# Three attentions of a decoder trunk's token mixer run as one sequence of 96 steps

## The reference, cut to what matters

```python
y_a = dsa_attention(...)              # keys chosen per query by an indexer's top-k (128 of 512)
y_b = rglru_branch(...)
y_c = mla_attention(...)              # causal, 96-wide heads
y_d = sliding_window_attention(...)   # window 128, a sink per head
ys = jnp.stack([y_a, y_b, y_c, y_d], axis=2)
proj = jnp.einsum('bsnw,nwd->bsnd', ys, w_branch)
g = jax.nn.sigmoid(gates.reshape(B, S, N_BRANCH, D_MODEL))
return jnp.sum(g * proj, axis=2) @ w_out
```

## Time and profile before

| what | value |
|---|---|
| median of 3 runs | 2865.91 us (2855.36 to 2866.02) |
| the profiled execution's own time | 2861.46 us |
| its span, first to last instruction | 2859.7 us |
| mean granted clock of TensorE, as a share of full speed | 0.995 |
| PE busy | 2749.6 us, 96% of the span |
| DVE busy | 1564.8 us, 55% |
| ACT busy | 1107.7 us, 39% |
| POOL busy | 272.9 us, 10% |

### The profile page before, as it was taken

The page is one execution under the profiler, slowest core; times in us unless marked ns, Lnnn a source line. Parts: engine busy times, 40 slices in busy tenths (PEclk is TensorE's granted clock), DMA queues, the critical chain, the costliest instruction groups (busy, mean ns, idle before and its releaser), DMA issues.

```text
span 2859.7 us, 37617 instructions
## 1 busy us (share of the span) xinstructions
PE 2749.6 (96%) x13312; PEld 2214.5 (77%) x13312; DVE 1564.8 (55%) x2636; ACT 1107.7 (39%) x2024; POOL 272.9 (10%) x360
## 2 busy tenths in 40 slices
PE   4999999998999999999999999999999999999999
PEld 4888888676767788888888888877666778888887
DVE  6655446767455647633266653567665466553323
ACT  2322234565454443222242222346555453432222
POOL 0111000112110001110011110001111000011100
PEclk9999999999999999999999999999999999999999
DMA  5655422111212224533335544221112223153332
GB/s 232 231 180 192 143 97 78 54 50 60 67 60 96 89 82 177 197 99 101 96 118 204 192 154 147 98 67 53 59 60 67 74 74 104 52 191 99 93 99 69
DMA packets 86252, 318.54 MB, mean 111 GB/s; under 512 B 9697, under 2 KB 10081, under 8 KB 84706
## 3 DMA queue, kind: packets, MB, share of 16 engines
q1 hardware_dynamic: 86114, 316.76, 32.5%
HBM read 314.62 MB, written 2.10 MB: 111 GB/s over the span
## 4 chain that ended last, share of the span: by engine, by line
PE 83%; DVE 7%; ACT 2%; issue 2%; DVEq 2%; DMA 2%; SPq 0%; POOL 0%; ACTq 0%; POOLq 0%
PE bank L453 19%; PE bank L454 19%; PE bank L455 19%; PE bank L462 6%; PE bank L460 6%; PE bank L461 6%; PE bank L1677 2%; PE bank L1661 1%; DVE w_low L437 1%; PE bank L1650 1%; DMA ada_raw<-ada 1%; PE bank L1642 1%; DVE scores_sb L1152 1%; DVEq L967 1%; ACT w_high L431 1%
## 5 line engine op out<-in xcount | busy, mean ns | idle before, releaser
L453 PE MATMUL bank<-h_high,w_high 128*128 128x512 f32 (+1 forms) x2528 | 976.8, 386 | 21.9 <-DVE h_low L1270 12.2
L455 PE MATMUL bank<-h_high,w_low 128*128 128x512 f32 (+1 forms) x2528 | 958.5, 379 | 0.0
L454 PE MATMUL bank<-h_low,w_high 128*128 128x512 f32 (+1 forms) x2528 | 958.4, 379 | 0.0
L437 DVE TENSOR_TENSOR w_low<-w_raw,w_high 128x1024 fp32r<-128x1024 f32 x437 | 565.8, 1296 | 654.2 <-ACT w_high L431 652.4
L431 ACT ACTIVATE w_high<-w_raw 128x1024 fp32r<-128x1024 f32 x437 | 458.6, 1051 | 356.1 <-PE bank L462 331.6
L453 PEld LDWEIGHTS bank<-h_high,w_high 128*128 128x128 f32 x2528 | 479.2, 190 | 126.2 <-issue 40.7
L455 PEld LDWEIGHTS bank<-h_high,w_low 128*128 128x128 f32 x2528 | 478.5, 189 | 89.6
L454 PEld LDWEIGHTS bank<-h_low,w_high 128*128 128x128 f32 x2528 | 478.6, 189 | 86.4 <-issue 2.4
L460 PE MATMUL bank<-w_high,ffn_high 128*128 128x512 f32 x704 | 275.6, 391 | 0.0
L462 PE MATMUL bank<-w_low,ffn_high 128*128 128x512 f32 x704 | 273.9, 389 | 0.0
L461 PE MATMUL bank<-w_high,ffn_low 128*128 128x512 f32 x704 | 273.9, 389 | 0.0
(11 more groups left out here) (194 smaller groups left out, 2716.7 us busy)
## 6 DMA issues: line engine op xcount, KB each, us to landing
w_raw<-stream SPq DMA_DIRECT2D x440, 512.0 KB, 3.6
ada_raw<-ada SPq DMA_DIRECT2D x128, 512.0 KB, 3.6
ada_start<-ada SPq DMA_DIRECT2D x8, 1024.0 KB, 17.2
mixer_consts<-mixc SPq DMA_DIRECT2D x2, 1152.0 KB, 5.1
x<-x_in SPq DMA_DIRECT2D x1, 2048.0 KB, 18.9
silu_c<-silu_row SPq DMA_DIRECT2D x4, 512.0 KB, 4.1
out<-x SPq DMA_DIRECT2D x8, 256.0 KB, 2.1
lru_w<-lruw SPq DMA_DIRECT2D x2, 512.0 KB, 3.8
```

The source lines that it names most:

```text
L437: eng.tensor_tensor(wL[:, slot], raw[:, slot], wH[:, slot].bitcast(F32), ALU.subtract).then_inc(lo_ready[slot].sem, 1)
L453: eng.matmul(o, a, rhs_h, start=first, stop=False)
L454: eng.matmul(o, a, rhs_l, start=False, stop=False)
L455: return eng.matmul(o, b, rhs_h, start=False, stop=last)
```

## The change

- The three attentions become one sequence, `("att", st)` with `st` from 0 to 100: 96 real steps (`NS`) and 5 in which the pipeline empties, in place of three times 37. `keys(g)` finds branch, block and head of step `g`.
- The filling is spread over three stretches of that sequence (steps 0 to 33, 34 to 67, 68 to 100), and the 48 top-k rounds over 84 steps (`TOPK_STEPS`), where 32 lay in the steps of C and 16 in those of D.
- The value transposes of D and A are items of the first filling and go to banks 2 and 3.
- On ACT the scaling of step `st`-1 comes ahead of the exponential of step `st`.
- The second product becomes an item of its own, `("pv", st)`, behind the filling of its step.

```diff
+NS = 3 * STEPS
+STEPS_ALL = NS - HEADS + Y_LAG + 1
+TOPK_STEPS = NS - HEADS - 4
-    def att(br, fill, topk=()):
-
-        fill, topk = list(halves(fill)), list(topk)
-        nf, nt = len(fill), len(topk)
+    def attention(fills, topk):
+
+        queue = [(a, b, len(items), list(items)) for a, b, items in fills]
+        topk = list(topk)
+        nt = len(topk)
         for st in range(STEPS_ALL):
-            yield ("att", br, st)
-            while topk and (nt - len(topk)) * STEPS < (st + 1) * nt:
+            yield ("att", st)
+            while topk and (nt - len(topk)) * TOPK_STEPS < (st + 1) * nt:
                 yield topk.pop(0)
-            while fill and (nf - len(fill)) * STEPS_ALL < (st + 1) * nf:
-                yield fill.pop(0)
+            for a, b, n, items in queue:
+                while items and (n - len(items)) * (b - a) < (st + 1 - a) * n:
+                    yield items.pop(0)
+            if PV_LAG <= st < NS + PV_LAG and (st - PV_LAG) % 2:
+                yield ("pv", st)
...
+    yield from attention([(0, STEPS + 2, [("vtok", "D"), *first, ("vtok", "A")]),
+                          (STEPS + 2, 2 * STEPS + 4, list(halves(merge("C")))),
+                          (2 * STEPS + 4, STEPS_ALL, third)], rounds)
...
+                    if 1 <= st < NS + 1:
+                        g = st - 1
+                        nk = keys(g)[4]
+                        s.wait_ge(recip_ready.sem, recip_ready.at(l, g + 1))
+                        s.activation(s_sb[:, g % S_SLOTS, 0:P * nk], s_sb[:, g % S_SLOTS, 0:P * nk], ACT.Copy,
+                                     scale=recip[:, g % 8:g % 8 + 1]).then_inc(norm_ready.sem, 1)
-                    if st < STEPS:
-                        g = att_index(br, st)
-                        b, h, k0, nk = keys(br, st)
+                    if st < NS:
+                        g = st
+                        br, b, h, k0, nk = keys(g)
                         c = 8 * (b % 2) + h
                         s.wait_ge(shifted.sem, shifted.at(l, g + 1))
...
-                    pe.wait_ge(pt_evicted.sem, pt_evicted.at(l, STEPS * (1 if br == "D" else 2)))
+                    pe.wait_ge(u_evicted.sem, u_evicted.at(l, U_BANK[("in", "ckv", 0)] + 1))
                     for tb in range(TB):
-                        mm = pe.transpose(bank[6][:, tb * P:(tb + 1) * P], src[:, tb * P:(tb + 1) * P], ident[:, :])
+                        mm = pe.transpose(bank[2 if br == "D" else 3][:, tb * P:(tb + 1) * P], src[:, tb * P:(tb + 1) * P], ident[:, :])
...
+        def tensor_values(pe, l, st):
+
+            g = st - PV_LAG
+            pair = g % HEADS // 2
+            pe.wait_ge(pt_evicted.sem, pt_evicted.at(l, g + 1))
+            if pair == 0 and g > 1:
+
+                pe.wait_ge(ylo_ready.sem, ylo_ready.at(l, g // HEADS))
```

More of the change, by code:

```diff
@@ L100, in mixer_schedule @@
     rounds = [("topk", b, r) for b in range(1, TB) for r in range(TOPK // 8)]
-    yield from att("C", [("in", "dq", j) for j in range(4)] + [("in", "aq", j) for j in range(4)] +
-                   [("in", "ak", 0), ("in", "av", 0)], rounds[:2 * (TOPK // 8)])
-    yield ("vtok", "D")
-    yield from att("D", merge("C"), rounds[2 * (TOPK // 8):])
-    yield ("vtok", "A")
-    yield from att("A", [*merge("D"), *[("in", "rx", j) for j in range(LRU_T)]])
+    first = list(halves([("in", "dq", j) for j in range(4)] + [("in", "aq", j) for j in range(4)] +
+                        [("in", "ak", 0), ("in", "av", 0)]))
+    third = list(halves([*merge("D"), *[("in", "rx", j) for j in range(LRU_T)]]))
+    yield from attention([(0, STEPS + 2, [("vtok", "D"), *first, ("vtok", "A")]),
+                          (STEPS + 2, 2 * STEPS + 4, list(halves(merge("C")))),
+                          (2 * STEPS + 4, STEPS_ALL, third)], rounds)
     yield from [("in", "rg", j) for j in range(LRU_T)]
@@ L555, in _, with keys, y_block @@
             sp.wait_ge(stored.sem, 16 * 2 * TB)
-        def att_index(br, st):
-            return STEPS * ATT.index(br) + st
-        def keys(br, st):
+        def keys(g):
+            br, st = ATT[g // STEPS], g % STEPS
             b, h = st // HEADS, HEAD_AT[br][st % HEADS]
             k0 = max(0, b - 1) if br == "D" else 0
-            return b, h, k0, b + 1 - k0
+            return br, b, h, k0, b + 1 - k0
+        def y_block(st):
+            return (st - Y_LAG) // HEADS if st >= Y_LAG and (st - Y_LAG) % HEADS == 0 else None
         @block.gpsimd
@@ L618, in _ @@
                                            ).then_inc(rs_ready.sem, 1)
-                        for br in ATT:
-                            for st in range(STEPS):
-                                reciprocals(l, br, st)
+                        for g in range(NS):
+                            reciprocals(l, g)
                         closing(l, 1)
@@ L1046, in vector_mixer @@
                 elif kind == "att":
[L1047 removed]
+                    vector_attention(v, l, it[1])
                 elif kind == "branch":
@@ L1121, in vector_mixer, with vector_attention @@
                     gains_0(l, 1)
-        def vector_attention(v, l, br, st):
-            ahead = [st] if br == "C" else [st, st + 1] if st % 2 == 0 else []
-            for st1 in ahead if st < STEPS else ():
-                g = att_index(br, st1)
-                b, h, k0, nk = keys(br, st1)
+        def vector_attention(v, l, st):
+            ahead = [st] if st < STEPS else [st, st + 1] if st % 2 == 0 and st < NS else []
+            for g in ahead:
+                br, b, h, k0, nk = keys(g)
                 w = P * nk
@@ L1153, in vector_attention @@
                                        ALU.min, nmax[:, c:c + 1]).then_inc(shifted.sem, 1)
-            blk = (st - Y_LAG) // HEADS
-            if st >= Y_LAG and (st - Y_LAG) % HEADS == 0:
-                g = TB * ATT.index(br) + blk
-                v.wait_ge(yhi_ready.sem, yhi_ready.at(l, g + 1))
-                cols = slice(blk * P, (blk + 1) * P)
-                i = Y_OF[br]
+            blk = y_block(st)
+            if blk is not None:
+                v.wait_ge(yhi_ready.sem, yhi_ready.at(l, blk + 1))
+                cols = slice(blk % TB * P, (blk % TB + 1) * P)
+                i = Y_OF[ATT[blk // TB]]
                 v.tensor_tensor(yL[i][:, :, cols], bank[7][:, :].rearrange("p (t n) -> p t n", t=4),
```

98 lines of the change are left out of this document (43 added, 55 removed).

## The result

| | before | with the change |
|---|---|---|
| median, us (lowest to highest) | 2863.65 (2855.36 to 2866.02), 4 runs | 2823.32 (2821.14 to 2825.37), 4 runs |
| ratio, 95% interval | | 0.9864 (0.9841 to 0.9888) |
| profiled execution, own time, span | 2861.46, 2859.7 | 2821.51, 2819.7 |
| granted clock, mean | 0.995 | 0.998 |
| the stretch, layer 1 and 2 | 361.9, 361.8 | 344.2, 344.5 |

What follows compares the result with a forecast made beforehand. PE, busy for 96% of the span, was taken as the bound, so only its idle time could go. Per layer 9.3 us of waits, 1.6 overlap and 1.6 clock, doubled: 25 us, giving 2837; own range 2825 to 2848, 8 in 10 2822 to 2855.

Steps and rivals of the forecast that it cites:

- R1: Rival: all PE idle in the stretch goes, and the clock's loss with it; 45 us gained, 2817; chance 0.08.
- (a): Second product's first pair of a block waiting for the output's low part: 5.4 of 7.4 us per layer go.
- (b): Transposes waiting for the copy of earlier ones out of their one bank: 2.7 of 6.6 us per layer go.
- (c): Scores waiting for the row minimum after empty odd steps: all 2.2 us per layer stay, nothing gained.
- (d): Second product waiting for a copy where a pipeline empties between attentions: 1.2 us per layer go.
- overlap at each wait: Matmul overlap of 0.16 us lost at each PE wait; ten waits fewer give 1.6 us per layer.
- clock: Eight matmuls at 0.43 us in place of 0.23 after a long wait; 1.6 us per layer goes.
- PE's own work stays: Same products, scores and transposes, 76 half units per layer, before and now; nothing gained or lost.
- (e): Scaling ahead of the exponential on ACT: costed at nothing; at most 15 us lost, or a small gain.
- R2: Rival: DVE sets the pace in D, more waits for the row minimum; gain 12 us, 2849; chance 0.14.
- R3: Rival: the reciprocal's round trip becomes ACT's pace and PE waits for it; 58 us cost, 2895; chance 0.04.
- R4: Rival: the low-part wait stays because the high part waits for the moved product; gain 9 us, 2852; chance 0.06.

Runs made afterwards that it cites:

- e1: The kernel before with only the second product moved behind its step's filling: 2832.74 us, ratio 0.9899.
- e5: The change with the top-k rounds early, one in each of the first 32 steps, then one in every second: 2822.83 us, ratio 0.9860.
- e12: The change with one top-k round in each of C's 32 steps, then one in every third step: 2824.93 us, ratio 0.9868.
- e2: The change with the second product put back ahead of the filling: 2855.98 us, ratio 0.9978.
- e11: e6 with one top-k round in each of C's 32 steps, then one in every third step: 2815.72 us, ratio 0.9838.
- e8: The kernel before, three sequences kept, with the second product behind the filling and the scaling ahead of the exponential: 2833.14 us, ratio 0.9887.
- e6: The change with the same 76 half units in other steps, so that no even step but step 0 is empty: 2823.49 us, ratio 0.9861.
- e10: The change with 32 top-k rounds in C, none in D and 16 in A's first 16 steps: 2836.45 us, ratio 0.9902.
- e4: The change with the second product back ahead of the filling and the scaling back behind the exponential: 2860.29 us, ratio 0.9992.
- e7: The kernel before with the second product ahead of the scores and transposes of its step: 2882.26 us, ratio 1.0064.
- e3: The change with the scaling back behind the exponential: 2829.81 us, ratio 0.9890.
- e9: e6 with 32 top-k rounds in C, none in D and 16 in A: 2828.21 us, ratio 0.9880.

## Why the prediction was right, and where its sum was short

Direction and place were right, and the measured time lies in the range of 8 in 10, but only just: it is 1.7 us under the forecast's own range (2825 to 2848), in the band that the prediction gave to R1 with a chance of 0.08. The sum, 12.5 us per layer, against 17.7 and 17.3 measured. The last three rows are the sums of starts of e1's section:

| step | forecast | measured, layer 1 |
|---|---|---|
| (a) low part | 7.4 to 2.0: 5.4 | 7.4 to 2.9: 4.5 |
| (b) one bank | 6.6 to 3.9: 2.7 | 6.6 to 3.4: 3.2 |
| (c) row minimum | stays: 0 | 2.2 to 0.3: 1.9 |
| (d) emptying | 1.2 | 1.2 |
| overlap at each wait | 10 waits: 1.6 | 11 waits: 0.9 |
| clock | 1.6 | 1.6 |
| order of groups on PE | not in the sum | 4.4 |

- **(a) was right in kind and in place.** e1 shows it alone: 7.4 to 0.4. Of the waits that stay, two make up nearly all: 0.75 us at step 45 and 2.01 at step 61, in the order of time. The prediction named steps 37 and 61 with 0.9 each, after the place of the earlier trace rows: step 37 has none, 45 was given 0.1, and 61 is twice as long. What the step left out are the rounds on 512 columns (1.46 us each) that the joined list puts into the odd steps 57 and 59, ahead of the low part that is made in step 60. With no round there (e5), or one (e12), all but 0.2 to 0.5 us is gone.
- **(b) was right in size**: 6 waits where 7 were counted, 0.6 us each, and the same with the product ahead (e2) or behind. The five of D and A came where they were counted. Of the two in C none came, and the sixth lies where C ends and D begins, which the count left out. The rule of the Trainium skill that the prediction weighed ("Perfetto Trace Analysis", Optimization Strategy), that a repeated gap can mean too little buffer, would have kept 6.6 us. The traces show 6.6, 3.4 and 0.2 us (before, change, e11, layer 1) with one and the same bank, as the empty even steps became fewer: too little buffer is not the only way to read such a gap. Whether a second bank would have done as much, no run shows.
- **(c) was taken at nothing and went.** It is there in e1 and e8 (2.1), with three sequences, and in none of the joined kernels with the rounds of the change and its filling (0.3 at most). The prediction held an empty odd step with DVE behind for the cause and counted five of them in D and at the start of A; there are six (33, 37, 47, 57, 61, 67), and none brings a wait in layer 1. The one that is left, 0.3 us, comes in step 32, behind the empty step 31. DVE's load in D stayed (72.4 us, 75.6 before). What spared the other steps was not isolated: e6, with other steps filled, has 4.0 us, and e10, with the filling of the change but rounds in A, has 5.1, so both filling and rounds decide it.
- **The clock** was right in size. The Trainium skill ("TensorE: Matmul & The Clock Gate", What's actually happening) puts the ramp at under 1% of a typical kernel's span, and the traces agree: half the time at the lower level is 12 us before, 0.4% of the span, 3.4 us of it in the stretches. But a model without it, which the prediction weighed, would have lost 3.3 of 35 us here. It would also have hidden the larger half of what scaling ahead brings and most of why e4 gives nothing (4.0 us per layer).
- **The overlap was sized at twice its worth.** The 0.16 us hold for transposes behind transposes; over the 11 waits that went it is 0.9 us in place of 1.8.
- **The step that failed is "PE's own work stays".** The work stays, but the time that it takes depends on what stands next to what: 4.4 us per layer. It was taken at nothing, and the distances between starts were not looked at. PE's busy time less what the lower clock cost it sorts the kernels by this alone: 341.8 to 342.8 us where the product stands ahead of the filling (before, e2, e4, e7), 335.6 to 338.6 where it stands behind (all the others). Why one neighbour costs more than another stays open.
- **(e), costed at nothing, was worth 6 us** in the two stretches: 6.1 behind the filling (e3 to the change), 6.5 ahead of it (e4 to e2), 3.2 without joining (e1 to e8). The prediction had the gain, "0.5 us by which a late minimum delayed the next copy", and stopped short of asking what else stands behind a scaling on ACT: a weight split, 0.4 us later, and through DVE the longest wait. A fall of the clock in each layer came with it, more than half of the 6 us.

ACT's new waits for the reciprocal are there, as forecast, in layer 1 (total, times, longest), and nobody waits for them:

```profile
ACT scores_sb L780 <- POOL recip L603: 9.2, 24, 0.7
```

Of the rivals, R1 gave the time nearest to the measured one (2817; the forecast was 2837), but not its reason: 6.6 us of waits stay. What brought the time there is the order of the groups, which neither had. R2 did not come, though DVE is busy for 75% of D now: waits for the minimum are 0.3 us. R3 fell, as no wait of PE with the change is for the scaling. R4 fell by e1: (a) is gone, though the high part waits for a product that was moved back. The sequence itself, 340 us before and forecast at 328, is 322.6 (524.4 to 847.0). Of the signs, the low part is over its bound (2.9 us, where under 2.5 was said), and the waits for the one bank are 0.3 to 0.9 us each in place of 0.5 to 0.6.

## What to carry to other kernels

Put work that needs a late answer behind a piece of other work, and do it first: this one move was worth four fifths of a change with five parts. Then place the filling where two users of one buffer would meet, and keep long work of a side engine away from the steps in which its answer is due: the joined order gave nothing alone (e4), and with the first move made, filling and rounds placed so gave 10 us more (e11). Compare the busy time of the bounding engine at an equal number of instructions, less what its clock cost: where it moves, order has a price that no list of waits shows. The distances between starts, by pair of neighbours, tell which.

## What the runs showed of the hardware

- **Neighbours on PE.** From the start of the last matmul of a group to the next start, at the full clock and without a wait: the second product (64 rows out, 128 columns) comes 0.20 us after a transpose, a matmul of 512 columns 0.04 us after it. After a matmul of 512 columns a transpose comes at 0.23, scores at 0.23 to 0.32 and the second product at 0.32. After the second product all of them come at 0.20. For a group of two transposes that is 0.31 to 0.34 us from its first start to the product, and 0.14 to 0.20 to 512 columns (before).
- **What a wait hides.** Beyond the shown idle a wait costs 0.05 to 0.07 us at most places and 0.16 where transposes wait behind transposes.
- **The clock.** In the stretches of all kernels it fell to its lower level at every wait of 2.54 us and more (up to 3.96 us, in e7). Of the shorter ones it fell at 2.38 us (e3, twice), 2.15 (before, and e10), 1.94 and 1.93 (e4) and 1.90 (e7). It did not at 2.52 and 2.43 (e10), 2.02 and 2.01 (the change), 1.91 (e7), nor at 2.47 in A before:

```profile
807.00:809.00 2.00, 1.43 (x15) 1.00 0.00 0
```

In e11 it fell behind a wait of 1.32 us, 2.5 us after one of 1.17; e6 and e9 have the same two waits without a fall. So the length of the wait alone does not decide it. A fall cost some 1.6 us, and at six of the waits from 2.95 to 3.96 us (e2, e4, e7, e9) the lower level lasted twice as long. A reader who prices a wait near 2 us or longer should add this as a risk. That bringing such a wait down to 2.0 us avoids it, no run shows.
